# Retention stage: scores made one query tile at a time, weights and values in high and low parts, gating in place

## The reference

```python
def odd_layer(x, g_norm, w_in, w_out):
    z = rms_norm(x, g_norm) @ w_in
    q, k, v, g = jnp.split(z, [qk_w, 2 * qk_w, 2 * qk_w + v_w], axis=-1)
    q = rotate(q.reshape(Bsz, S, N_HEADS_RET, RET_QK_DIM))
    k = rotate(k.reshape(Bsz, S, N_HEADS_RET, RET_QK_DIM)) * (RET_QK_DIM ** -0.5)
    y = retention(q, k, v.reshape(Bsz, S, N_HEADS_RET, RET_V_DIM))
    y = head_group_norm(y).reshape(Bsz, S, v_w).astype(x.dtype)
    return x + (y * jax.nn.silu(g)) @ w_out
```

## Time and profile before

| | |
|---|---|
| median of three runs | 3934.26 us (3933.34 to 3938.03) |
| the profiled execution | 3938.19 us, span 3936.4 us |
| PE, PEld busy | 3625.0 us (92%), 2946.5 us (75%) |
| DVE, ACT, POOL busy | 1722.5 us, 1310.4 us, 1361.6 us |
| mean granted TensorE clock | 0.954 |
| weighing, L2614 | 144 float32 matmuls, 288 passes |
| scores, L2590 | 96 float32 matmuls, 192 passes |

### The profile page before, as it was taken

One profiled execution on the slowest core, in us unless ns is written; L12 is line 12 of the kernel. 1 busy time (PEld: TensorE's weight loads), 2 busy tenths in 40 slices (PEclk: granted clock), 3 DMA queues, 4 the chain that ended last, 5 costly groups with the idle time before them and its releaser, 6 DMA issues. The chain is left out here.

```text
span 3936.4 us, 47774 instructions
## 1 busy us (share of the span) xinstructions
PE 3625.0 (92%) x17072; PEld 2946.5 (75%) x17072; DVE 1722.5 (44%) x3164; ACT 1310.4 (33%) x2413; POOL 1361.6 (35%) x797
## 2 busy tenths in 40 slices
PE   5997787889999996999999999997898999999797
PEld 4776666778888885788888888886777776868486
DVE  4666455243333335355565565555314323241422
ACT  3777243010111112355555665555101202021210
POOL 3120210232333331466556666665223121313031
PEclk8998788989999997999999999998999999999898
DMA  3000200311111103352333442220513120202141
GB/s 96 22 6 6 52 31 16 98 50 49 50 49 50 50 27 85 39 60 49 49 56 51 34 41 36 38 38 17 176 37 108 33 68 24 75 23 69 59 155 70
DMA packets 201811, 210.75 MB, mean 54 GB/s; under 512 B 12432, under 2 KB 156048, under 8 KB 201632
## 3 DMA queue, kind: packets, MB, share of 16 engines
q1 hardware_dynamic: 179760, 148.85, 17.6%
q10 hardware_dynamic: 21872, 59.32, 4.2%
HBM read 176.62 MB, written 31.52 MB: 53 GB/s over the span
## 5 line engine op out<-in xcount | busy, mean ns | idle before, releaser
L520 PE MATMUL ps<-all_u_hi,kept_w_hi 128*128 128x512 f32 x1824 | 733.1, 402 | 19.3 <-POOL kept_w_lo L475 14.2
L524 PE MATMUL ps<-all_u_hi,kept_w_lo 128*128 128x512 f32 x1824 | 716.3, 393 | 0.0
L523 PE MATMUL ps<-all_u_lo,kept_w_hi 128*128 128x512 f32 x1824 | 715.0, 392 | 0.0
L473 POOL CAST kept_w_hi<-kept_w_raw 128x1024 fp32r<-128x1024 f32 x122 | 135.6, 1111 | 1498.6 <-PE ps L520 851.8
L1172 POOL TENSOR_SCALAR even_probs<-even_probs,even_stat 128x128 f32<-128x128 f32 (+7 forms) x256 | 451.8, 1772 | 307.4 <-DVE even_stat L1588 306.9
L520 PEld LDWEIGHTS ps<-all_u_hi,kept_w_hi 128*128 128x128 f32 x1824 | 348.0, 191 | 83.5 <-POOL kept_w_lo L475 14.3
L524 PEld LDWEIGHTS ps<-all_u_hi,kept_w_lo 128*128 128x128 f32 x1824 | 345.9, 190 | 74.7
L523 PEld LDWEIGHTS ps<-all_u_lo,kept_w_hi 128*128 128x128 f32 x1824 | 346.9, 190 | 63.4
L1593 DVE TENSOR_TENSOR even_probsT_lo<-ps,even_probsT_hi 128x512 fp32r<-128x512 f32 (+3 forms) x384 | 196.1, 552 | 262.2 <-ACT even_probsT_hi L1428 261.2
L475 POOL TENSOR_TENSOR kept_w_lo<-kept_w_raw,kept_w_hi 128x1024 fp32r<-128x1024 f32 x122 | 302.0, 2475 | 9.8
L1419 ACT ACTIVATE even_probs<-even_probs,even_stat 128x128 f32<-128x128 f32 (+7 forms) x256 | 199.0, 778 | 301.8 <-DVE even_stat L1582 301.8
(11 more groups left out here) (418 smaller groups left out, 7398.1 us busy)
## 6 DMA issues: line engine op xcount, KB each, us to landing
kept_w_raw<-in_even_w_in_dram SPq DMA_DIRECT2D x64, 512.0 KB, 8.3
kept_w_raw<-in_odd_w_in_dram SPq DMA_DIRECT2D x48, 512.0 KB, 3.7
kept_w_raw<-in_w_up_dram SPq DMA_DIRECT2D x16, 512.0 KB, 4.0
mlp_w_raw<-in_w_up_dram SPq DMA_DIRECT2D x16, 512.0 KB, 4.0
kept_w_raw<-in_w_down_dram SPq DMA_DIRECT2D x16, 512.0 KB, 3.5
mlp_w_raw<-in_w_down_dram SPq DMA_DIRECT2D x16, 512.0 KB, 3.5
scratch_h<-residual SPq DMA_DIRECT2D x2, 4096.0 KB, 18.9
even_bias<-scratch_negc ACTq DMA_DIRECT2D x16, 512.0 KB, 6.4
```

Source lines behind the costliest of these rows:

```text
L473: nc.gpsimd.tensor_copy(w.hi[:, s, :], w.raw[:, s, :]).then_inc(w_hi.sem, 1)
L520: ins = nc.tensor.matmul(dst, lh, rh, start=first, stop=False)
L523: nc.tensor.matmul(dst, lh, rl, start=False, stop=False)
L524: return nc.tensor.matmul(dst, ll, rh, start=False, stop=last)
```

## The change

- v is kept as VH (ACT's copy, type fp32r) and VL (DVE: PSUM minus VH). `wide` now waits for DVE's half instead of ACT's.
- Scores are made for one query tile at a time: `scores(j)` takes the 128 queries of tile j as the streamed operand and each key tile 0 to j as stationary one, so 2 (j + 1) float32 matmuls of 128 columns each. The blocks are stored by distance d.
- The decayed scores go to DS (DVE), from there to WH (ACT, `weights_hi`) and WL (DVE, `weights_lo`), two buffers each. On ACT, `weights_hi(0)` and `weights_hi(1)` stand behind the whole gate chain; on DVE, `weights_lo(0)` and `weights_lo(1)` stand behind `gate(3)`, the later ones behind the normed tile.
- The weighing is three fp32r matmuls (`product`) for each block instead of one float32 matmul, and waits for the low parts (`split_lo`) instead of `decayed`.
- The gated result overwrites the gate GT instead of going to yT; ACT waits for the last store before it copies a new gate.

Core of the diff:

```diff
@@ matmul queue
-                            pe.wait_ge(dense_out.sem, dense_out.at(16 * it + TOKENS.index(n) + 1))
+                            pe.wait_ge(v_out_dve.sem, v_out_dve.at(TT * it + TOKENS.index(n) + 1))
...
-                        n = (TT - j) * P
-                        for c0 in range(0, n, HALF):
-                            c1 = min(c0 + HALF, n)
+                        at = slice(j * P, j * P + P)
+                        for d in range(j + 1):
+                            key = slice((j - d) * P, (j - d) * P + P)
                             for i in range(2):
-                                last = nc.tensor.matmul(S[j % 2][:, c0:c1], K[:, i, j * P:j * P + P],
-                                                        Q[:, i, j * P + c0:j * P + c1], start=i == 0, stop=i == 1)
+                                last = nc.tensor.matmul(S[j % 2][:, d * P:d * P + P], K[:, i, key], Q[:, i, at],
+                                                        start=i == 0, stop=i == 1)
...
-                        pe.wait_ge(decayed.sem, decayed.at(TT * it + i + 1))
+                        pe.wait_ge(split_lo.sem, split_lo.at(TT * it + i + 1))
...
-                        for j in range(i + 1):
-                            at = off[j] + (i - j) * P
-                            last = nc.tensor.matmul(ps[:, 6 + i % 2, :], PA[:, at:at + P], V[:, j, :],
-                                                    start=j == 0, stop=j == i)
+                        for d in range(i + 1):
+                            at = slice(d * P, d * P + P)
+                            last = product(ps[:, 6 + i % 2, :], (WH[:, i % 2, at], WL[:, i % 2, at]),
+                                           (VH[:, i - d, :], VL[:, i - d, :]), d == 0, d == i)
@@ ACT
-                        nc.scalar.activation(V[:, t, :], ps[:, t, :], ACT.Copy).then_inc(dense_out.sem, 1)
+                        nc.scalar.activation(VH[:, t, :], ps[:, t, :], ACT.Copy).then_inc(dense_out.sem, 1)
+                    act.wait_ge(stored.sem, stored.at(16 * it))
...
+                    def weights_hi(i):
+                        n = (i + 1) * P
+                        act.wait_ge(decayed.sem, decayed.at(TT * it + i + 1))
+                        if i >= 2:
+                            act.wait_ge(pv_done.sem, pv_done.at(TT * it + i - 1))
+                        nc.scalar.activation(WH[:, i % 2, 0:n], DS[:, i % 2, 0:n], ACT.Copy).then_inc(split_hi.sem, 1)
+
+                    weights_hi(0)
+                    weights_hi(1)
...
+                        if i + 2 < TT:
+                            weights_hi(i + 2)
@@ DVE
+                    for i, t in enumerate(TOKENS):
+                        dve.wait_ge(dense_out.sem, dense_out.at(16 * it + i + 1))
+                        nc.vector.tensor_tensor(VL[:, t, :], ps[:, t, :], VH[:, t, :].bitcast(F32), ALU.subtract)\
+                            .then_inc(v_out_dve.sem, 1)
...
-                    def decay(j):
-                        n = (TT - j) * P
+                    def decay(i):
+                        n = (i + 1) * P
...
+                    def weights_lo(i):
+                        n = (i + 1) * P
+                        dve.wait_ge(split_hi.sem, split_hi.at(TT * it + i + 1))
+                        nc.vector.tensor_tensor(WL[:, i % 2, 0:n], DS[:, i % 2, 0:n], WH[:, i % 2, 0:n].bitcast(F32),
+                                                ALU.subtract).then_inc(split_lo.sem, 1)
...
                     decay(0)
                     decay(1)
                     gate(NV - 1)
-
-                    dve.wait_ge(stored.sem, stored.at(16 * it))
+                    weights_lo(0)
+                    weights_lo(1)
```

More of the change, by code:

```diff
@@ L2501, in retention_stage @@
         TOKENS = (0, 2, 1, 3, 4, 6, 5, 7)
-        V = sb("v", [P, TT, RET_V])
+        VH, VL = sb("v_hi", [P, TT, RET_V], FR), sb("v_lo", [P, TT, RET_V], FR)
         GT = sb("gT", [P, NV, SEQ])
         GE = sb("ge", [P, SEQ])
-        yT = sb("yT", [P, NV, SEQ])
-        off = [sum((TT - i) * P for i in range(j)) for j in range(TT + 1)]
-        PA = sb("weights", [P, off[TT]])
+        WH, WL = sb("weights_hi", [P, 2, SEQ], FR), sb("weights_lo", [P, 2, SEQ], FR)
+        DS = sb("decayed", [P, 2, SEQ])
         DEC = sb("decay", [P, SEQ])
@@ L2657, in _ @@
                         nc.scalar.activation(st[:, 10:11], st[:, 9:10], ACT.Exp, scale=-0.5).then_inc(root.sem, 1)
+                        if i + 2 < TT:
+                            weights_hi(i + 2)
                     act.wait_ge(y_out.sem, y_out.at(TT * it + TT))
-                    act.dma_start(YT[bass.ds(it * NV, NV), :, :].rearrange("a p t -> p a t"), yT[:])\
+                    act.dma_start(YT[bass.ds(it * NV, NV), :, :].rearrange("a p t -> p a t"), GT[:])\
                         .then_inc(stored.sem, 16)
@@ L2700, in _ @@
                     dve.wait_ge(table_in.sem, table_in.at(16 * it + 16))
-                    def decay(j):
-                        n = (TT - j) * P
-                        dve.wait_ge(scores_ready.sem, scores_ready.at(TT * it + j + 1))
-                        nc.vector.tensor_tensor(PA[:, off[j]:off[j] + n], S[j % 2][:, 0:n], DEC[:, 0:n], ALU.mult)\
+                    def decay(i):
+                        n = (i + 1) * P
+                        dve.wait_ge(scores_ready.sem, scores_ready.at(TT * it + i + 1))
+                        nc.vector.tensor_tensor(DS[:, i % 2, 0:n], S[i % 2][:, 0:n], DEC[:, 0:n], ALU.mult)\
                             .then_inc(decayed.sem, 1)
+                    def weights_lo(i):
[3 more added lines that the diff above has]
+                                                ALU.subtract).then_inc(split_lo.sem, 1)
                     def gated_out(i):
@@ L2710, in gated_out @@
                         dve.wait_ge(y_turned.sem, y_turned.at(TT * it + i + 1))
-                        nc.vector.tensor_tensor(yT[:, :, at], ps[:, 4 + i % 2, :].rearrange("p (v c) -> p v c", c=P),
+                        nc.vector.tensor_tensor(GT[:, :, at], ps[:, 4 + i % 2, :].rearrange("p (v c) -> p v c", c=P),
                                                 GT[:, :, at], ALU.mult).then_inc(y_out.sem, 1)
@@ L2747, in _ @@
                             .then_inc(normed.sem, 1)
+                        if i + 2 < TT:
+                            weights_lo(i + 2)
                         if i >= 1:
@@ L2759, in retention_stage @@
         gate_step.close(2 * NV * R_)
-        for m in (scores_ready, decayed, pv_done, ln_done, root, normed, y_turned, y_out):
+        for m in (v_out_dve, split_hi, split_lo, scores_ready, decayed, pv_done, ln_done, root, normed, y_turned, y_out):
             m.close(TT * R_)
```

## The result

The changed kernel takes 3943.6 us (median of 15 runs, 3939.17 to 3948.69); the kernel before, in 15 runs by now, takes 3937.1 us (3930.18 to 3941.56). The ratio is 1.0019, 95% interval 1.0011 to 1.0027, that is 4 to 11 us more. The profiled execution of the changed kernel took 3939.17 us, span 3937.2. That is the shortest of its 15 and only 0.8 us longer in span than the one before: it reached the first score matmul at 3105.08, the one before at 3112.39, in code that the change does not touch. What the change costs must be read round by round.

The account below looks back on a forecast made before the run. PE was taken to bound the retention stage: 50.4 us a round plus 2.3 of lost clock make 52.7 against 50.48, +8.9 us over four rounds. On the median 3934.26 that gives 3943.2 us, range 3932 to 3951.

Parts of the forecast that it names:

- The bound: Retention stage: PE sets the time, busy 49.60 of 50.48 us per round in the part the change rewrites.
- The weighing: Weighing blocks: three fp32r products cost 0.68 us instead of 0.86, saving 6.4 us per round.
- rival (e): Weighing: three matmuls with changing accumulation cost more than dense ones; break-even 0.286 us each, there 3968 us; chance 0.02.
- The narrow scores: Scores by query tile: 144 passes of 128 columns at 0.111 us, 16.0 us, half a us more per round.
- rival (c): Narrow scores in long runs: weight loads bind at 0.17 us a pass, +8.5 us per round, 3977 us; chance 0.02.
- The wait: Before each round's first weighing: PE stands 6.8 us behind the gate chain and starts weighing at 8.1 us.
- The old wait of 0.88: PE's 0.88 us wait per round for the first normed tile, predicted to disappear.
- rival (b): Tiles 2 to 4: DVE becomes the bound, 1 to 2 us more per round, 3947 to 3951 us; chance 0.08.
- Without the clock: Retention round at full clock: 50.4 us against 50.48, the weighing's saving spent in the new wait.
- The clock: After the new wait: clock falls to 0.50 for 4.55 us, losing 2.3 us per round.
- rival (a): Retention rounds: the clock does not fall, or only now and then; 3934 us, bounds 3932 to 3937; chance 0.12.
- The sum: Whole kernel: rounds of 52.7 us against 50.48, +8.9 us over four, set on median 3934.26: 3943.2 us.

Follow-up runs that it names:

- The three products alone: Kernel before with only the three-product weighing and in-place gating, scores by key tile, weights' high part standing in for the low: 3915.77 us against 3936.85.
- the wait filled with matmuls: Changed kernel with 26 unneeded fp32r matmuls in the wait before each round's first weighing: 3936.95 us against 3936.52 for the kernel before.
- the second comparison: The changed kernel, unedited, timed again beside the kernel before: 3945.95 us against 3936.52, ratio 1.0031.
- scores by query tile alone: Changed kernel without halves and three products, weights and values float32, scores by query tile and in-place gating kept: 3963.42 us against 3936.52 for the kernel before.
- the fastest version: Changed kernel with first halves and scores of tiles 0 and 1 moved ahead, last gate chain behind the first tile's root: 3908.51 us against 3936.98 before.

## Why the prediction was right, point by point

- The bound. "So in this stage PE sets the time" held: every edit came out as what it did to PE's issue and waits.
- The weighing. 0.68 us a block, 6.4 us less a round, was forecast. The three products alone gave 5.6, or 6.1 without the longer wait. So the term of 6.4 was 0.3 too large. Most of that is the distance between the matmuls: in the last tile of the kernel after they stand (3343.02 - 3337.75) / 23 = 0.229 us apart, where 0.227 was taken, 0.25 us over 108 matmuls; that is far from the 0.286 of rival (e). The first matmul after the transposes needs 0.31 us to the next one (3337.44 to 3337.75), but the four transposes ahead of it take 0.35 (from 3337.09) instead of 0.44, which gives that back.
- The narrow scores. 0.111 was taken against the rule of the Trainium skill ("TensorE: Matmul & The Clock Gate", section "Weight-path perf modes — Fast Weight Load (FWL) and DoubleRow") that would make the loads of float32 weights bind: 0.112 in runs of 32, so rival (c) is out. Whether the fast load was off, no run shows.
- The wait. The weighing was forecast at 8.1 us and starts at 8.02; each step of the gate chain is within 0.05 us of the one that was read off the chain of j = 2. "The old wait of 0.88 goes" held, and rival (b) never appeared: PE has no gap after the first weighing.
- Without the clock. 50.4 was the sum, 50.66 the measurement (the wait filled with matmuls).
- The clock. It fell in every round of both profiled executions, so rival (a) is out. The size was taken as 4.55 us at the low clock and 2.3 us of loss, with 3.9 to 5.7 as bounds. PE worked 2.9 to 5.6 us at the low clock and rounds lost 1.3 to 2.6 us against 50.66; the lower bound was too high, because seven other places of the trace were too few to bound it. Filling the wait put the cost at about 9 us for the four rounds by time, 5 to 8 by the two traces, which are of short executions.
- The sum. +8.9 us was forecast; the ratios give +7.5 (4.3 to 10.6) and, in the second comparison, +12 (7.5 to 16.5). The predicted 3943.2 beside the measured 3943.6 is closer than the working earns, and that is luck: the forecast difference was 1.4 to 2.4 us too large against this comparison, and the median of three on which the difference was set, 3934.26, lies 2.8 us under the later median of 15. The forecast of "slower by over 0.2%" as likelier than not, 0.57, was about an even matter, and the measured 0.19% is at that line.
- The rest. The low half of v, the waits for the store and the gating in place cost nothing: the dense stretch has 120.50 us, before 120.51.

## What to carry to other kernels

Before matmuls are made cheaper or shorter, ask what else their time covered: here two wide score tiles hid a gate chain on two other queues, and without them a gain of 6 us a round turned into a wait of the same size. New small operations that PE will wait for belong ahead of long chains that nobody waits for; with two small copies put ahead of the end of a gate chain, and its last three operations put behind, a loss of 7 to 12 us became a gain of 22. Price a wait of several us on PE twice, once as idle time and once as the matmuls at the low clock behind it, and after each wait that is removed look at which queue makes the next one (a 0.2 us root behind 3 us of gate work).

## What the runs showed of the hardware

- An idle time of 3.83 us in the middle of dense matmuls was enough to bring the granted clock to 0.50 in all four rounds (scores by query tile alone); idle times of 1.38 us and less left it at 1.00.
- Between these two lies the idle time of 2.96 to 2.97 us before the last four transposes of the fourth round, which every version has. In the kernel before the transposes behind it ran at a clock of 0.50 (3715.30 to 3716.40) and took 1.12 us; in the fastest version they ran at 1.00 (3686.40 to 3687.00) and took 0.66. The same idle time can go either way. The two rows, kernel before first:

```profile
3715.28 1.12 PE L2599 MATMUL ps<-all_ident,ret_yn 128*128 128x128 f32 x4 [2.97 <-DVE ret_yn L2746]
...
3686.32 0.66 PE L2598 MATMUL ps<-all_ident,ret_yn 128*128 128x128 f32 x4 [2.96 <-DVE ret_yn L2790]
```

- The same idle time, 6.52 us, cost different amounts in different rounds, 1.3 to 2.6 us, since the clock came back 2.9 to 5.6 us after PE resumed.
- float32 passes of 128 columns, each with a weight load recorded as 0.19 us, ran 0.112 us apart for 32 in a row (kernel after, 3328.26 to 3331.83).
